# Layer 0 of a hybrid decoder on one core: the SiLU chain started from the third z step on, sums of squares behind a dense tile, one weight pair loaded during the heads, stores reordered

## What is computed

```python
def conv_module(za, prev_rows, conv_w, conv_b, ln_g, ln_b):
    u = za[..., :D_CONV] * jax.nn.sigmoid(za[..., D_CONV:])
    u_ext = jnp.concatenate([prev_rows.astype(u.dtype), u], axis=1)
    y = ...  # depthwise convolution of 31 taps, plus conv_b
    y = jax.nn.silu(layer_norm(y, ln_g, ln_b))
    return y, u_ext[:, -(CONV_WIDTH - 1):]

def gla_mixer(zq, zk, zv, zg, zr, s0, w_gate, b_gate, g_norm):
    ...
    o, s_new = gla_chunked(q, ..., s0.astype(f32))
    o = rms_norm(o, g_norm) * jax.nn.silu(heads(zg, GLA_HV))

# per layer: y = y + gate * (concat(ya, yb) @ w_out); y = y + gate * swiglu(modulate(y))
```

## Time and profile before

| | us |
|---|---|
| median of 3 runs | 2785.71 (2785.27 to 2792.23) |
| profiled execution, its own time | 2784.97 |
| its span, first to last instruction | 2783.2 |
| PE busy / DVE busy / ACT busy / POOL busy | 2686.3 / 1426.3 / 1159.6 / 95.6 |
| granted TensorE clock, mean | 0.983 |
| DMA, mean over the span | 217 GB/s |

### The profile page before, as it was taken

One profiled execution on the slowest core, in us unless ns is written; L12 is line 12 of the kernel. 1 busy time (PEld: TensorE's weight loads), 2 busy tenths in 40 slices (PEclk: granted clock), 3 DMA queues, 4 the chain that ended last, 5 costly groups with the idle time before them and its releaser, 6 DMA issues.

```text
span 2783.2 us, 48514 instructions
## 1 busy us (share of the span) xinstructions
PE 2686.3 (97%) x20155; PEld 2479.9 (89%) x20155; DVE 1426.3 (51%) x1983; ACT 1159.6 (42%) x1521; POOL 95.6 (3%) x136
## 2 busy tenths in 40 slices
PE   5899998999999999999999999998999999999998
PEld 1688987778989888989999899998999999999998
DVE  1589946554444433444444556666454444445444
ACT  2433245444343322334443546535444433444433
POOL 1100011110000000000000000001000000000000
PEclk7999999999999999999999999999999999999999
DMA  9977764587777788777455454344554455455453
GB/s 392 368 291 268 282 236 134 163 354 268 291 263 283 271 318 337 284 273 276 162 225 166 135 195 137 102 130 167 165 162 161 145 162 187 166 165 163 137 165 127
DMA packets 110042, 603.61 MB, mean 217 GB/s; under 512 B 24829, under 2 KB 26301, under 8 KB 53578
## 3 DMA queue, kind: packets, MB, share of 16 engines
q1 hardware_dynamic: 109898, 601.56, 60.9%
HBM read 592.02 MB, written 9.49 MB: 216 GB/s over the span
## 4 chain that ended last, share of the span: by engine, by line
PE 87%; DMA 6%; DVE 3%; ACT 2%; issue 1%; SPq 0%; DVEq 0%; ACTq 0%
PE ps L863 26%; PE ps L865 25%; PE ps L864 25%; PE ps L1069 5%; DMA pre_ring<-in_w_ada 3%; DMA aring<-in_w_ada 2%; ACT w_hi L1380 1%; DVE w_lo L1848 1%; DMA raw<-in_w_dn 1%; PE ps L1082 1%; PE ps L1051 0%; PE ps L1037 0%; PE ps L1219 0%; PE ps L1039 0%; PE ps L1038 0%
## 5 line engine op out<-in xcount | busy, mean ns | idle before, releaser
L1848 DVE TENSOR_TENSOR w_lo<-raw,w_hi 128x2048 fp32r<-128x2048 f32 (+2 forms) x410 | 804.2, 1962 | 1039.5 <-ACT w_hi L1380 1039.4
L863 PE MATMUL ps<-act_hi,w_hi 128*128 128x288 f32 x4128 | 1233.9, 299 | 8.2 <-DVE w_lo L1848 4.5
L864 PE MATMUL ps<-act_hi,w_lo 128*128 128x288 f32 x4128 | 1219.4, 295 | 0.0
L865 PE MATMUL ps<-act_lo,w_hi 128*128 128x288 f32 x4128 | 1215.1, 294 | 0.0
L1380 ACT ACTIVATE w_hi<-raw 128x2048 fp32r<-128x2048 f32 (+2 forms) x410 | 673.8, 1644 | 1062.9 <-PE ps L865 1044.7
L863 PEld LDWEIGHTS ps<-act_hi,w_hi 128*128 128x128 f32 x4128 | 775.3, 188 | 62.5 <-issue 55.8
L865 PEld LDWEIGHTS ps<-act_lo,w_hi 128*128 128x128 f32 x4128 | 778.7, 189 | 0.0
L864 PEld LDWEIGHTS ps<-act_hi,w_lo 128*128 128x128 f32 x4128 | 776.8, 188 | 0.0
L863 PE MATMUL ps<-hid_hi,w_hi 128*128 128x288 f32 x1408 | 418.8, 297 | 0.7 <-DVE w_lo L1848 0.7
L864 PE MATMUL ps<-hid_hi,w_lo 128*128 128x288 f32 x1408 | 415.4, 295 | 0.0
L865 PE MATMUL ps<-hid_lo,w_hi 128*128 128x288 f32 x1408 | 414.0, 294 | 0.0
(11 more groups left out here) (329 smaller groups left out, 1770.7 us busy)
## 6 DMA issues: line engine op xcount, KB each, us to landing
raw<-in_w_gu SPq DMA_DIRECT2D x172, 1024.0 KB, 5.3
aring<-in_w_ada SPq DMA_DIRECT2D x168, 1024.0 KB, 6.9
raw<-in_w_dn SPq DMA_DIRECT2D x128, 704.0 KB, 4.1
raw<-in_w_ab SPq DMA_DIRECT2D x40, 1024.0 KB, 6.6
raw<-in_w_out SPq DMA_DIRECT2D x64, 512.0 KB, 4.0
raw<-in_w_cd SPq DMA_DIRECT2D x26, 1024.0 KB, 5.2
pre_ring<-in_w_ada SPq DMA_DIRECT2D x16, 1024.0 KB, 10.6
aring<-in_state_glaT SPq DMA_DIRECT2D x4, 1024.0 KB, 7.4
```

Source lines behind the costliest of these rows:

```text
L863: pe.matmul(bank, w_hi[:, h, cols], hi[:, kt, :], start=begin, stop=False)
L864: pe.matmul(bank, w_lo[:, h, cols], hi[:, kt, :], start=False, stop=False)
L865: mm = pe.matmul(bank, w_hi[:, h, cols], lo[:, kt, :], start=False, stop=end)
L1848: dve.tensor_tensor(w_lo[:, h, 0:w], raw[:, par, h * KT * P:h * KT * P + w], w_hi[:, h, 0:w].bitcast(F32), ALU.subtract).then_inc(split_do ...
```

## The change

Five things move. No arithmetic changes.

- **z segment.** SP issues the pair of a step's end behind the next step's weights. ACT and DVE run `conv_silu(0)` to `conv_silu(2)` at step 2, and at step 3 the rest of the chain ahead of `a_high(0)`, `a_high(1)` and `double_copy`.
- **Heads 0 to 2 on PE.** `conv_half(4h + 3)` stands ahead of the product that sums squares. ACT follows: `a_evict(4h + 3)` ahead of `make_rstd`, and the values of the next head ahead of `a_high(4h + 5)`. DVE weights `sg` ahead of the state updates.
- **Last head.** DVE splits the second half of the first out step (`split_lo(..., 1)`) behind the head's output instead of ahead of it.
- **SP in the mixer.** The eight `conv_s` stores are issued in heads 0 and 1, four in each. In head 2, behind the last conv weights, SP loads pair 20 (`HELD`) into `side`.
- **Out segment.** The pairs stand at steps 1, 2, 4 and 6. SP issues pair 21, then pair 25, ahead of the weights of step 2. Pair 24 follows the use of pair 20, and pairs 22 and 23 are issued at steps 3 and 5.

```diff
+HELD = MIX_PAIRS
+SIDE_PAIRS = HELD, 24, 25, 77, 78
-    segs += ["mix0", Seg("out", 0, 4, 2, 0, MIX_PAIRS, (1, 3, 5, 6), group=1), norm]
+    segs += ["mix0", Seg("out", 0, 4, 2, 0, MIX_PAIRS, (1, 2, 4, 6), group=1), norm]
...
@@ SP, body
-                    for p in (pair_of(seg, ls), pair_at_end(seg, ls)):
-                        if p is not None:
-                            load_pair(p)
-                    if seg is OUT0 and ls in (4, 6):
-                        sp.wait_ge(half_done, 2 * seg.n0 + 4)
-                        sp.wait_ge(conv_stored, 16 * (CT + 1))
-                        load_pair(UNDER_NORM[1][ls // 2 - 2])
+                    if seg is OUT0:
+                        if ls == 0:
+                            load_pair(HELD + 1)
+                            sp.wait_ge(gla_y, HEADS)
+                            sp.wait_ge(side_landed[1], 32)
+                            load_pair(UNDER_NORM[1][1])
+                        if ls == 2:
+                            sp.wait_ge(ada_used, 4 * PRE + 2 * HELD + 2)
+                            load_pair(UNDER_NORM[1][0])
+                        if ls in (3, 5):
+                            load_pair(HELD + (ls + 1) // 2)
+                    else:
+                        for p in (pair_at_end(seg, ls - 1), pair_of(seg, ls)):
+                            if p is not None:
+                                load_pair(p)
@@ SP, mix0
-                    for j in (2 * h, 2 * h + 1):
+                    for j in range(4 * h, 4 * h + 4) if h < 2 else ():
                         sp.dma_start(o["conv_s"][:, j], rows_s(j)[:, :, TS:SW]).then_inc(conv_stored, 16)
+                    if h == HEADS - 2:
+                        sp.wait_ge(conv_stored, 16 * (CT + 1))
+                        sp.wait_ge(a_done, 1)
+                        load_pair(HELD)
@@ PE, mix0
+                    if h < HEADS - 1:
+                        conv_half(4 * h + 3)
                     pe.wait_ge(osq_ready, h + 1)
...
                     mm.then_inc(ms_ready, 1)
-                    conv_half(4 * h + 3)
+                    if h == HEADS - 1:
+                        conv_half(4 * h + 3)
@@ ACT, body (DVE alike, with a_low)
-                    elif nxt is OUT0 and end:
-                        a_high(0)
-                        a_high(1)
-                    elif nxt:
+                    elif nxt and not (nxt is OUT0 and end):
                         split(nxt, n + 1, 1 - par, 0)
...
-                    if ends_double(seg, ls):
+                    if ends_double(seg, ls) and not (seg.kind == "z" and end):
                         double_copy(pair_of(seg, ls) // 4)
...
-                        for k in range(2):
+                        for k in range(3):
                             conv_silu(k)
                     if seg.kind == "z" and ls == 3:
-                        for k in range(2, CT // 2 + 1):
+                        for k in range(3, CT // 2 + 1):
                             conv_silu(k)
+                        a_high(0)
+                        a_high(1)
+                        double_copy(pair_of(seg, ls) // 4)
@@ ACT, mix0
                     act.activation(sqb[:], ps[:, 2:4, 0:T], ACT.Square).then_inc(osq_ready, 1)
+                    if not last:
+                        a_evict(4 * h + 3)
                     act.wait_ge(ms_ready, h + 1)
                     make_rstd(256, la).then_inc(gla_rs, 1)
                     if last:
                         split(after, after.n0, after.n0 % 2, 1)
-                    a_evict(4 * h + 3)
-                    if not last:
+                        a_evict(4 * h + 3)
+                    else:
+                        values_to_tok(h + 1)
                         a_high(4 * h + 5)
-                        values_to_tok(h + 1)
@@ DVE, mix0
+                    dve.wait_ge(gsig_ready, h + 1)
+                    for b in range(2):
+                        ...  # sg weighted with g_norm, moved up from behind the state updates
+                    weighted = L.mark(ins)
                     dve.wait_ge(gla_yy, h + 1)
                     dve.wait_ge(snew_ready, h + 1)
...
-                    if h == HEADS - 1:
-                        split_lo(after, after.n0, after.n0 % 2, 1)
...
                     if h < HEADS - 1:
                         a_low(4 * h + 5)
+                    else:
+                        split_lo(after, after.n0, after.n0 % 2, 1)
```

More of the change, by code:

```diff
@@ L48 @@
 UNDER_NORM = {1: (24, 25), 2: (77, 78, 79)}
-SIDE_PAIRS = 24, 25, 77, 78
+HELD = MIX_PAIRS
+SIDE_PAIRS = HELD, 24, 25, 77, 78
 DOUBLES = [8, 10, 16, 18, 12, 14] + list(range(20, 48, 2))
@@ L367, in build @@
         with ExitStack() as a:
-            sb("under_side", [P, 4800], stack=a)
+            sb("under_side", [P, 24 * T - 8 * ADA_N], stack=a)
             side = sb("side", [P, 2, 2, 4 * ADA_N], stack=a)
@@ L474, in unit_of @@
             n = 4 * ADA_N
-            if p in UNDER_NORM[1]:
-                return side[:, p - UNDER_NORM[1][0], r]
+            if p == HELD or p in UNDER_NORM[1]:
+                return side[:, 0 if p == UNDER_NORM[1][1] else 1, r]
             if p in SIDE_PAIRS:
@@ L480, in unit_of, with side_of, side_bytes @@
             return aring[:, r, :]
-        def norm_of(p):
-            return next(k for k in UNDER_NORM if p in UNDER_NORM[k])
+        def side_of(p):
+            return 1 if p == HELD else next(k for k in UNDER_NORM if p in UNDER_NORM[k])
+        def side_bytes(p):
+            return {HELD: 32, 24: 96, 25: 96}.get(p, 64)
         def norm_pairs(seg):
@@ L612, in load_pair @@
                     if p in SIDE_PAIRS:
-                        sp.dma_start(unit_of(p, r), rows).then_inc(side_landed[norm_of(p)], 16)
+                        sp.dma_start(unit_of(p, r), rows).then_inc(side_landed[side_of(p)], 16)
                         continue
@@ L1060, in ada_pair @@
                 if p in SIDE_PAIRS:
-                    pe.wait_ge(side_landed[norm_of(p)], 64)
+                    pe.wait_ge(side_landed[side_of(p)], side_bytes(p))
                 else:
@@ L2033, in body @@
                             split_lo_behind_restart(nxt, n + 1, 1 - par)
-                        elif nxt is OUT0 and end:
-                            a_low(0)
-                            a_low(1)
-                        else:
+                        elif not (nxt is OUT0 and end):
                             split_lo(nxt, n + 1, 1 - par, 0)
@@ L2044, in body @@
                         if seg.kind == "z" and ls == 2:
-                            for k in range(2):
+                            for k in range(3):
                                 conv_silu(k)
                         if seg.kind == "z" and ls == 3:
-                            for k in range(2, CT // 2 + 1):
+                            for k in range(3, CT // 2 + 1):
                                 conv_silu(k)
+                            a_low(0)
+                            a_low(1)
                         if seg.kind == "sgu" and ls == 0:
@@ L2272, in mix0 @@
                         split_lo(after, after.n0, after.n0 % 2, 0)
+                    dve.wait_ge(gsig_ready, h + 1)
+                    for b in range(2):
+                        gn = VEC["gla_g_norm"] + b
+                        ins = dve.scalar_tensor_tensor(sg[:, b], z[:, 16 + 2 * h + b, :], vec[:, gn:gn + 1], sg[:, b],
+                                                       ALU.mult, ALU.mult)
+                    weighted = L.mark(ins)
                     dve.wait_ge(gla_yy, h + 1)
@@ L2282, in mix0 @@
                         ins.then_inc(snew_used, 1)
-                    if h == HEADS - 1:
-                        split_lo(after, after.n0, after.n0 % 2, 1)
-                    dve.wait_ge(gsig_ready, h + 1)
-                    for b in range(2):
-                        gn = VEC["gla_g_norm"] + b
-                        ins = dve.scalar_tensor_tensor(sg[:, b], z[:, 16 + 2 * h + b, :], vec[:, gn:gn + 1], sg[:, b],
-                                                       ALU.mult, ALU.mult)
-                    L.link(ins)
+                    L.wait(weighted)
                     dve.wait_ge(gla_rs, h + 1)
```

## The result

The changed kernel takes 2772.95 us in the median (2771.56 to 2775.14, four runs); the kernel before, in the same comparison, 2788.23 us (2785.27 to 2792.23). The ratio is 0.9937, with a 95% interval of 0.9925 to 0.9949: 0.63% or 17.6 us less (14.2 to 20.9), well outside the 0.3% that can be told from no change. The forecast was 2767.2 us in a range of 2759 to 2777, and a gain of 18.5 us against the kernel before. The profiled execution took 2771.56 us, its span 2769.8 us, at a granted clock of 0.986 (0.983 before).

A forecast was written before the change was run, and what follows sets the result against it. PE was busy 97% of the span, so only its idle time and clock could be won. The terms -4.45 - 5.35 - 3.15 - 1.65 - 10.0 + 6.8 - 0.7 gave -18.5 us, from 2785.71 to 2767.2 us, range 2759 to 2777.

The forecast's parts named there:

- A: z segment: weights go out ahead of pair 18, which lands 2.95 us earlier, and 1.5 us of clock return; -4.45 us.
- B: z end: k = 2 moves to step 2, the SiLU chain ahead of a_high; conv_half(1) 9.8 us early; -5.35 us.
- The cover that I called thin: z end: last half's split ends near 405.0 us, PE wants it at 405.5; without cover each us shows on PE.
- C: Heads 0 to 2: squares' 4.4 us of waits not counted; clock won in heads 1 and 2, 2 x 1.58; -3.15 us.
- the clock is not won back: Rival: short waits at the z end and in the heads still lower the clock; 2773 us, chance 0.15.
- D: Last head: the split and sg leave the path ahead of act_lo, for which PE waits 1.83 us; -1.65 us.
- E: Out segment: pairs issued a step or more ahead remove 6.5 us of waits and 3.5 us of clock loss; -10.0 us.
- F: Third out step: weights behind pairs 21 and 25 cost 5.3 us of wait, then 1.5 us of clock; +6.8 us.
- no new wait, or a short one: Rival on the third out step: F between 0 and +3; 2760.4 to 2763.5 us, chance 0.17.
- the queue stays the bound: Rival: out segment runs behind the two pairs put first, E's 10 us do not come; 2777.2 us, chance 0.09.
- G: Norm: pair 26's 1.40 us wait behind a full queue halves, as two weight slots still go first; -0.7 us.
- slower: Rival: in the heads the clock sticks at 1.2 GHz; two such heads make 2812 us; chance 0.03.

The follow-up runs named there:

- high_first: The changed kernel with a_high(0), a_high(1), double_copy and a_low back ahead of the SiLU chain at the last z step: ratio 0.9946 to the kernel before.
- the second profile: The changed kernel measured once more, with nothing changed: 2773.04 us, ratio 0.9934 to the kernel before.
- w_first: The changed kernel with the third out step's weights issued ahead of both pairs 21 and 25: ratio 0.9914 to the kernel before.
- w_second: The changed kernel with the third out step's weights issued between pairs 21 and 25: ratio 0.9919 to the kernel before, 0.9913 in its repeat.
- late24: The changed kernel with the third out step's weights between pairs 21 and 25, and pair 24 issued two steps later: ratio 0.9911 to the kernel before.
- outpart: The kernel before with only the pairs and the conv_s stores of the out segment changed: ratio 0.9983.
- sg_late: The changed kernel with the weighting of sg put back behind the state updates on DVE: ratio 0.9943 to the kernel before.
- z_order: The kernel before with only SP's order in the z segment changed, a step's end pair behind the next step's weights: ratio 0.9990.
- heads: The kernel before with only the heads' order changed on PE, ACT and DVE, the last head's split included: ratio 0.9996.

## Why the prediction was right, step by step

**A, pair order in z (-4.45): right.** Pair 18 at 388.78 in before's frame (389.15 - 0.37), forecast 388.7, with 0.97 us of wait (0.9). Pair 19 follows 14.85 us later (14.9 forecast, 16.40 before), so the clock's 1.5 us came too: it starts 4.4 us early.

**B, the z end (-5.35): right.** `conv_half(1)` at 421.87 in the same frame, forecast 421.9. The bias's wait turned into 0.96 + 1.69 us for `act_lo` (about 3 foreseen). A and B together are -9.8 in both profiles. high_first shows that the order gives 3.6 of these, clock included. The cover that I called thin held: pair 19 and the last half have no wait.

**C, the heads (-3.15): right in size, in part by luck.** The squares' 4.4 us of wait vanished and were not won, as forecast. Head 1 takes 26.00 and 25.97 us at a clock of 1.00 (27.74 at 0.94 before). Head 2 did not win its clock back in either profile of the changed kernel: 26.84 and 26.53 us at 0.94 (27.66 at 0.94 before), which the prediction had named as a sign of being wrong. The timeline of the second profile:

```profile
476.18 0.40 PE L1236 MATMUL ps<-act_hi,w_hi 128*128 128x288 f32 x1 [0.54 <-DVE w_lo L1876]
...
502.71 0.40 PE L1236 MATMUL ps<-act_hi,w_hi 128*128 128x288 f32 x1 [0.54 <-DVE w_lo L1876]
```

Heads 0 to 2 together take 78.8 and 78.4 us for 81.6, a gain of 2.8 and 3.1. Two errors met: DVE's new order made every head 0.2 us shorter, and half of head 2's clock stayed lost. In w_first, both profiles of w_second and late24, whose code is the same up to there, head 2 reads 1.00, and the three heads gain 3.6 to 3.7 us. So the rival *the clock is not won back* holds for head 2 in some executions; what decides it in one execution is open.

**D, the last head (-1.65): right as far as it shows.** The 1.83 us for `act_lo` at the start of the out segment are gone; outpart, which has not this part, still has them (1.8). sg_late puts 0.8 us of them back.

**E, pairs in the out segment (-10.0), and F, the new wait (+6.8): right in kind, each too large.** The pairs' 6.5 us of wait are gone. The third step's wait is 4.51 us, forecast 5.3, and 24 matmuls behind it take 4.74 us (539.83 to 544.57) where 3.46 are usual: 1.3 us of clock. So F is 5.8 us by the rows, and w_first, w_second and its repeat give back 4.8 to 5.8. From 538 to 623 us the changed kernel gains 3.5 us, where E, F and G say 3.9; w_second, which has no F, gains 8.7 there, so E with G is -8.7 and not -10.7, and F by this difference 5.2. The windows of PE between these two marks, in the kernel before, the changed one and w_second:

```profile
538.48:623.45 84.97, 75.69 (x542) 0.96 0.85 336
524.53:605.98 81.45, 74.39 (x544) 0.98 0.85 334
523.50:599.80 76.30, 72.96 (x544) 1.00 0.89 357
```

The clock was won back whole (what is low in the changed kernel follows F's wait), but in w_second that is 2.7 us of busy time and not the 3.5 of the forecast; and PE's idle time shrank by 5.9 us where 7.2 were forecast, since w_second still waits 0.74 us at pair 22 and 0.6 us for `act_lo` at the norm. The errors in E and F are of opposite sign, and that their sum came out is luck. F's landing was 14.67 us for 4.72 MB where I had 15.1. The Trainium skill ("DMA: Bandwidth & Descriptors", Anatomy of one DMA) fits 2.0 us plus bytes at 436 GB/s to one DMA issued from GpSimd, which the prediction did not say; for these groups from SyncE that would be, as an estimate, 12.8 us for 4.72 MB and 8.0 for w_second's 2.62. The rows have 14.7 and 10.1: the time per byte is near the fit's, the fixed part 2 us longer. The Trainium skill ("DMA: Bandwidth & Descriptors", Queues, rings and completion order) has each DMA engine consume descriptors in ring order, and the runs agree: with the 2.10 MB of pair 25 out of the way the same weights came 4.6 us sooner. The rival *no new wait, or a short one* falls with this, and so does *the queue stays the bound*.

**G, the norm (-0.7): right.** 0.78 us for 1.40.

**The sum** was -18.5 us; the profiles have -17.9 and -18.1 behind the norm, the ratios -17.6 and -18.4. Its parts agree too: of the terms, 7.8 us net are clock (1.5 in A, 1.15 in B, 3.15, 3.5, less 1.5 in F) and 10.7 are waits; the rows of the changed stretch have 7.4 of busy time and 10.4 of idle time. The *slower* rival, the clock stuck low, did not appear in any of the profiles.

**What failed: "behind the norm PE is gapless for hundreds of us, so nothing gives it back".** Two things do, and each profile has both. From the norm to the end the first profile loses 4.1 us, 2.9 of busy time (2132.2 us for 2129.3, clock) and 1.1 of idle time; the second 4.2 us, 1.6 and 2.5. The idle time is waits for pairs in the gate-up steps: PE's waits from 623 to 1300 us are 1.6 and 3.0 us (0.4 in the same view of before). Neither part is tied to the change. z_order and heads, whose code there is the old one, wait 3.6 and 3.0 us for pairs there and lose 6.3 and 4.1 us in all; w_second has no such wait and loses 0.6 us, its repeat has 4.0 us of them and loses 6.3. Every one of the thirteen other profiles is later over this stretch than that of the kernel before, which was one of the quick ones: its 2784.97 us is 3 to 7 us under the medians of the same kernel (2788.23, 2791.07, 2791.53, 2791.35; the last three from the later comparisons, on chips 5, 2 and 2). So most of the 4 us are probably the reference profile's luck, and the 13.4 us between the two single profiles too little. This is inferred: the kernel before was profiled once. It also bears on the absolute time. Of the 5.7 us between 2767.2 and 2772.95, 2.5 lie in the start from 2785.71 where the fourth run made it 2788.23, and 0.9 in the gain (18.5 against 17.6); the rest is what medians of four runs and their ratio differ by.

## What to carry to other kernels

Cost a wait by who sets the cycle: 4.4 us of waits on PE were worth nothing in themselves here, 0.93 us on DVE was worth 0.85, and a new 0.7 us wait on PE was free. But look at the clock beside it: with the heads' old order head 1 reads 0.94 in all four profiles, with the new order 1.00 in all ten, and that was 1.5 us. Whether the waits or the small matmuls around them bring the clock down, no run separates. When an upstream stage is made faster, move the loads of the next stage in the same change, or its gain is paid back as waits for them; and of several loads that can go out at one point, put the one that is wanted first in front, even ahead of a pair that was late before. Compare two single profiles only up to the mark where the change ends, and take the total from paired runs.

## What the runs showed that I had not expected

- A pair in front costs its bytes at the full rate: 2.10 MB more took 14.67 - 10.06 = 4.61 us more, 456 GB/s by the difference of two profiles. The row below has 418 at a share of 0.99, and the stage as a whole moves 331 at a share of 0.85. The fixed part in front of that is, as an estimate, some 4 us (10.06 less 2.62 MB at 456 GB/s is 4.3), more than the 3.1 us that I had taken from the earlier trace rows.
- The granted clock is 1.00 in heads 0 and 1 with their waits of 0.70 and 0.55 us, and at the z end with 0.96 and 1.69 us. In head 2 the same waits stand, and it reads 0.94 in five of the ten profiles with the new order, the two of the changed kernel among them, and 1.00 in the other five. After 4.51 us it read 0.67 over the next 4.74 us, between its two levels of 1.2 and 2.4 GHz:

```profile
539.83:544.57 4.74, 4.74 (x24) 0.67 0.99 418
```

- The code behind the norm differs by 5.7 us between two executions of the same kernel (w_second), and the start of the program by 4.6 us between two kernels that share it (w_second and w_first). That is more than most single steps of this change, and the reason why z_order, heads and late24 could be read in their profiles and hardly in their times.
